# A fill tile per token block between late levels of the triangular solver, instead of behind the right-hand sides

## The reference

```python
def step(state, inp):                       # rwkv7_scan
    r_t, w_t, k_t, v_t, a_t, b_t = inp
    sa = jnp.einsum('bhij,bhj->bhi', state, a_t)
    state = (state * w_t[:, :, None, :] + sa[..., None] * b_t[:, :, None, :]
             + v_t[..., None] * k_t[:, :, None, :])
    return state, jnp.einsum('bhij,bhj->bhi', state, r_t)

m = jnp.where(strict, jnp.einsum('bnhid,bnhjd->bnhij', k_beta, k) * decay_mat, 0.0)
t_inv = lax.linalg.triangular_solve(eye + m, jnp.broadcast_to(eye, m.shape), left_side=True,
                                    lower=True, unit_diagonal=True)   # chunk_gated_delta_rule
```

## Time and profile before

| | us |
|---|---|
| median of three runs | 3095.12 (3090.31 to 3096.48) |
| the profiled execution, own time | 3103.75 |
| its span | 3100.7 |
| TensorE matmuls busy | 2743.8 (88% of the span) |
| VectorE busy | 1880.1 (61%) |
| ScalarE busy | 1342.8 (43%) |
| mean granted TensorE clock | 0.925 of full speed |

### The profile page before, as it was taken

One profiled execution on the slowest core, in us unless ns is written; L12 is line 12 of the kernel. 1 busy time (PEld: TensorE's weight loads), 2 busy tenths in 40 slices (PEclk: granted clock), 3 DMA queues, 4 the chain that ended last, 5 costly groups with the idle time before them and its releaser, 6 DMA issues. The chain is left out here.

```text
span 3100.7 us, 58400 instructions
## 1 busy us (share of the span) xinstructions
PE 2743.8 (88%) x25404; PEld 2336.9 (75%) x25404; DVE 1880.1 (61%) x2644; ACT 1342.8 (43%) x1882; POOL 87.9 (3%) x120
## 2 busy tenths in 40 slices
PE   7887778999887688999998888889999988978899
PEld 6776656888776657898887775678888877757788
DVE  5755766975765766956656444656565655446564
ACT  5413334655413244645453232544454532325453
POOL 0020000000110000000000200000000011000000
PEclk9897889999997889999998888989999988889999
DMA  5211114564211123554542121335655421113353
GB/s 222 96 43 55 69 56 149 192 214 174 83 59 52 69 96 136 203 196 165 203 152 103 42 71 40 112 138 201 221 179 203 151 77 56 69 41 130 143 199 128
DMA packets 54686, 386.48 MB, mean 125 GB/s; under 512 B 6688, under 2 KB 7328, under 8 KB 8352
## 3 DMA queue, kind: packets, MB, share of 16 engines
q1 hardware_dynamic: 54432, 382.76, 34.7%
HBM read 381.69 MB, written 1.05 MB: 123 GB/s over the span
## 5 line engine op out<-in xcount | busy, mean ns | idle before, releaser
L321 PE MATMUL banks<-normed_high,weights_high 128*128 128x256 f16 (+1 forms) x4096 | 1141.6, 279 | 42.7 <-DVE weights_low L307 20.1
L322 PE MATMUL banks<-normed_low,weights_high 128*128 128x256 f16 (+1 forms) x4096 | 1140.2, 278 | 0.0
L323 PE MATMUL banks<-normed_high,weights_low 128*128 128x256 f16 (+1 forms) x4096 | 1139.7, 278 | 0.0
L307 DVE SCALAR_TENSOR_TENSOR weights_low<-weight_ring,weights_high 128x2048 f16<-128x2048 f32 x334 | 761.2, 2279 | 406.3 <-ACT weights_high L301 391.9
L301 ACT ACTIVATE weights_high<-weight_ring 128x2048 f16<-128x2048 f32 x306 | 580.2, 1898 | 274.8 <-PE banks L323 262.6
L321 PE MATMUL banks<-projected,weights_high 128*128 128x256 f16 x1696 | 472.3, 278 | 72.4 <-DVE projected L332 72.4
L321 PEld LDWEIGHTS banks<-normed_high,weights_high 128*128 128x128 f16 (+1 forms) x4096 | 409.7, 100 | 121.7 <-issue 30.2
L322 PE MATMUL banks<-projected,weights_high 128*128 128x256 f16 x1696 | 472.7, 279 | 0.0
L323 PE MATMUL banks<-projected,weights_low 128*128 128x256 f16 x1696 | 472.2, 278 | 0.0
L323 PEld LDWEIGHTS banks<-normed_high,weights_low 128*128 128x128 f16 (+1 forms) x4096 | 408.5, 100 | 55.8
L322 PEld LDWEIGHTS banks<-normed_low,weights_high 128*128 128x128 f16 (+1 forms) x4096 | 408.6, 100 | 55.5 <-issue 1.3
(11 more groups left out here) (398 smaller groups left out, 3021.2 us busy)
## 6 DMA issues: line engine op xcount, KB each, us to landing
weight_ring<-w SPq DMA_DIRECT2D x356, 1024.0 KB, 4.8
small_weights<-small SPq DMA_DIRECT2D x2, 1280.0 KB, 7.3
constants<-const SPq DMA_DIRECT2D x1, 1601.0 KB, 10.1
weight_ring<-w SPq DMA_DIRECT2D x2, 640.0 KB, 3.8
residual<-xt SPq DMA_DIRECT2D x1, 1024.0 KB, 4.8
small_weights<-small SPq DMA_DIRECT2D x2, 512.0 KB, 10.4
out<-residual SPq DMA_DIRECT2D x4, 256.0 KB, 2.5
parameters<-par SPq DMA_DIRECT2D x2, 115.5 KB, 9.4
```

The lines of the kernel that those rows point to most:

```text
L307: nc.vector.scalar_tensor_tensor(out=self.part(self.mem.w_low, g), in0=self.part(self.mem.ring, g), scalar=W_SCALE, in1=self.part(self.mem ...
L321: pe.matmul(out, w_high, high, start=start, stop=False, skip_group_check=skip)
L322: pe.matmul(out, w_high, low, start=False, stop=False, skip_group_check=skip)
L323: return pe.matmul(out, w_low, high, start=False, stop=stop, skip_group_check=skip)
```

## The change

In all four stages, one fill tile per block leaves its place in the chain behind the solver and goes between two levels of the solver: tile 2 (n = 0) and tile 6 (n = 1), in rwkv behind level 4 in both blocks, in delta behind level 5 for n = 0 and behind level 4 for n = 1. These tiles now use PSUM bank 6 instead of 0. ScalarE copies them out from inside its part of the solver (behind level 5, in delta n = 0 behind level 6), and TensorE waits for these copies (`fill_out` 3 and 7) before the right-hand sides take bank 6. Behind `rhs` in rwkv, behind `new` in delta n = 0 and behind the seen part in delta n = 1 there is now no fill tile.

```diff
--- before.py
+++ after.py
@@ -1582,12 +1582,12 @@
                 say(A(bonus[:, i, :], bonus[:, i, :], ACT.Identity, bias=col("gn_b", i)),
                     "bonus_shifted")
             out(1)
-            solver.scalar(act, nc, sig, 0, {3: [high(3)]})
-            out(2, 3)
+            solver.scalar(act, nc, sig, 0, {3: [high(3)], 5: [lambda: out(2)]})
+            out(3)
             high(4)()
             out(4, 5)
-            solver.scalar(act, nc, sig, 1, {2: [lambda: norm.root(act, nc, say, 1)], 3: [high(5)]})
-            out(6)
+            solver.scalar(act, nc, sig, 1, {2: [lambda: norm.root(act, nc, say, 1)], 3: [high(5)],
+                                            5: [lambda: out(6)]})
             high(6)()
             out(7)
             norm.root(act, nc, say, 2)
@@ -1642,8 +1642,11 @@
                 solver.tensor(pe, sig, n, {0: [lambda pe: need("near_seen", 2),
                                                lambda pe: fill.tensor(pe, sig, 5)],
                                            "growth": [lambda pe: need("fill_out", 6)],
+                                           4: [lambda pe: fill.tensor(pe, sig, 6)],
                                            5: [lambda pe: norm.turn(pe, 1, TURN_BANK[0])]} if n
-                              else {"growth": [lambda pe: need("fill_out", 2)]})
+                              else {"growth": [lambda pe: need("fill_out", 2)],
+                                    4: [lambda pe: fill.tensor(pe, sig, 2)]})
+                need("fill_out", (3, 7)[n])
                 if n:
                     need("turned_read", 1)
 
@@ -1654,7 +1657,6 @@
                         mm = pe.matmul(o, p_k[hp(h), h % 4, b1], state[hp(h), h % 4, :],
                                        start=False, stop=True)
                 mm.then_inc(sig("rhs_summed"), 1)
-                fill.tensor(pe, sig, (2, 6)[n])
                 need("rhs", n + 1)
                 need("t_ready", 2 * len(LEVELS) * (n + 1))
                 for h in range(HEADS):
@@ -2765,14 +2767,15 @@
                     out(0, 1)
                     say(A(flat(y_out), flat(dz), ACT.Sigmoid), "z_sigmoid")
                     high(2)()
-                    solver.scalar(act, nc, sig, n, {2: [high(3)]})
-                    out(2, 3)
+                    solver.scalar(act, nc, sig, n, {2: [high(3)], 6: [lambda: out(2)]})
+                    out(3)
                     high(4)()
                 else:
                     out(4, 5)
                     solver.scalar(act, nc, sig, n, {2: [high(5)],
-                                                    3: [lambda: norm.root(act, nc, say, 1)]})
-            out(6, 7)
+                                                    3: [lambda: norm.root(act, nc, say, 1)],
+                                                    5: [lambda: out(6)]})
+            out(7)
             high(6)()
             norm.root(act, nc, say, 2)
             out(8, 9, 10, 11, 12, 13)
@@ -2790,6 +2793,7 @@
             for n in range(NBLK):
                 if n:
                     need("state", 1)
+                    need("fill_out", 3)
 
                 for s in range(HEADS):
                     o = ps[:, 2 + s // 4, (s % 4) * P:(s % 4 + 1) * P]
@@ -2809,23 +2813,25 @@
                 for i in ((0, 1), (4, 5))[n]:
                     fill.tensor(pe, sig, i)
                 need("fill_out", (2, 6)[n])
-                solver.tensor(pe, sig, n, {5: [lambda pe: norm.turn(pe, 1, TURN_BANK[0])]} if n
-                              else {})
+                solver.tensor(pe, sig, n, {4: [lambda pe: fill.tensor(pe, sig, 6)],
+                                           5: [lambda pe: norm.turn(pe, 1, TURN_BANK[0])]} if n
+                              else {5: [lambda pe: fill.tensor(pe, sig, 2)]})
                 if n:
                     need("turned_read", 1)
+                    need("fill_out", 7)
                     for s in range(HEADS):
                         mm = pe.matmul(ps[:, 6 + s // 4, (s % 4) * HD:(s % 4 + 1) * HD],
                                        kh[hp(s), s % 4, :], state[hp(s), s % 4, :],
                                        start=True, stop=True)
                     mm.then_inc(sig("seen_summed"), 1)
-                    fill.tensor(pe, sig, 6)
                 need("rhs", 2 * (n + 1))
                 need("t_ready", 2 * len(LEVELS) * (n + 1))
                 for s in range(HEADS):
                     mm = pe.matmul(ps[:, 4, s * HD:(s + 1) * HD], tt[:, s, :],
                                    rhs[:, s * HD:(s + 1) * HD], start=True, stop=True)
                 mm.then_inc(sig("new_summed"), 1)
-                fill.tensor(pe, sig, (2, 7)[n])
+                if n:
+                    fill.tensor(pe, sig, 7)
                 need("new", n + 1)
                 for s in range(HEADS):
                     o = ps[:, 4 + s // 4, (s % 4) * HD:(s % 4 + 1) * HD]
@@ -2859,8 +2865,8 @@
 
 
 AHEAD = 2
-RWKV_BANKS = (3, 2, 0, 2, 2, 3, 0, 2, 1, 3, 0, 2, 1)
-DELTA_BANKS = (0, 1, 0, 0, 0, 1, 0, 1, 2, 3, 0, 1, 2, 3)
+RWKV_BANKS = (3, 2, 6, 2, 2, 3, 6, 2, 1, 3, 0, 2, 1)
+DELTA_BANKS = (0, 1, 6, 0, 0, 1, 6, 1, 2, 3, 0, 1, 2, 3)
 HGRN_SLOTS = (2,) + (1, 1, 0) * 2 + (1, 0, 0, 2, 1)
 DSA_SLOTS = (4,) + (1, 0, 0) * 4
 FOX_SLOTS = (1, 1, 0) * 4
```

## The result

The changed kernel took 3113.1 us (median of seven runs, 3111.3 to 3118.1); seven runs of the kernel before took 3102.6 (3090.3 to 3104.0). The ratio is 1.0048 (95% interval 1.0035 to 1.0062), some 15 us slower; forecast were 13.6. The two medians stand only 10.5 us apart, for the seven runs of before fall into two groups, three at 3090.3 to 3096.5 and four at 3102.6 to 3104.0; the ratio lies between what either group alone would give (19 and 10 us). The two profiled executions stand 15.5 us apart: span 3116.2 us after and 3100.7 before, mean granted clock 0.922 and 0.925.

What follows compares the result with a forecast made beforehand. TensorE was taken as the bound, by its own rate or a TensorE-ScalarE-VectorE chain, its varying clock mattering most. Terms -8.0 + 25.4 - 1.8 - 2.0 = +13.6 us gave 3108.7 us; eight-in-ten range 3096 to 3119.

Steps and rivals of the forecast that it cites:

- Tiles out, tiles in: Eight fill tiles leave their places behind the right-hand sides, -32.6 us; put between solver levels they cost +14.5 us.
- Waits: Behind the right-hand sides TensorE now waits uncovered for VectorE's copy: 1.06 us in six blocks, 1.87 in two; +10.1 us.
- The half clock carried on: Clock lost around level 6 returns only in tile 3 or 7, slowing T·rhs, state and that tile; 29.2 us, weighed +25.4.
- The weight of 0.87: Factor on the 29.2 us of carried half clock, for blocks that do not fall or fall later; gives +25.4 us.
- L2825 at full clock in half of the cases: Delta n = 0: with the tile directly ahead of level 6, these 16 matmuls may run at full clock; -1.8 us.
- the pairs L2797/L2799: Delta: a later clock rise lets more of the 16 pairs run fast; 4.8 us per stage at most, -2.0 us taken.
- the clock falls where it fell: Rwkv and delta n = 1: a whole level separates new tile and level 6, so the fall does not move.
- Constant clock: Rival: the fall no longer reaches T·rhs or costs nothing new; +3.6 us, 3098.7 us; chance 0.13.
- The late fill holds the clock: Rival: a tile nearer level 6 keeps the clock up through the right-hand sides; -20 us in all eight blocks; chance 0.10.
- VectorE takes the bound: Rival: behind `rhs`, one more low half is uncovered in four n = 1 blocks; +9 us on top, 3118 us; chance 0.11.
- The rule of the Trainium skill: Long idle gaps between matmul bursts drop the clock, continuous busy time restores it; no gap here would be long enough.
- the second rival: "The late fill holds the clock"; argued against because level 6 read 1.0 in two rows, the clock falling only behind it.

Runs made afterwards that it cites:

- delta_only: The change made in the two delta stages alone, rwkv as in the kernel before; 3102.0 us, ratio 1.0015 to the kernel before.
- rwkv_only: The change made in the two rwkv stages alone, delta as in the kernel before; 3106.1 us, ratio 1.0028 to the kernel before.
- next_first: Changed kernel with tile 3 or 7 moved one step forward, into the place that tiles 2 and 6 had; 3115.3 us, ratio 1.0056 to the kernel before.
- dummy_tile: Changed kernel plus 24 unused matmuls of a fill tile's shape in each of the eight old tile places; 3116.6 us, ratio 1.0063 to the kernel before.
- three_tiles: Kernel before with a third tile inside each n = 1 block, ahead of level 5, and one tile less at the block's end; 3101.7 us, ratio 1.0011.
- after_hold: Changed kernel plus five unused matmuls in each of level 6's two holes and eight in the uncovered wait; 3109.2 us, ratio 1.0037 to the kernel before.

## Why the prediction was right

The mechanism was right: a half clock carried on from the right-hand sides to the next tile. Its sum goes through the trace of the kernel after as follows, each line over the eight blocks.

*Tiles out, tiles in.* -32.6 us holds for this pair of traces, being read from before. It is no typical value: the first block's 5.12 us was 2.62 in delta_only with the same program. The new tiles took 2.72 us from their start to that of the level (862.12 to 864.85), all eight at full clock and none late for its weights or bank; +14.5 as forecast.

*Waits.* 0.85 us of idle TensorE, and the tile used to begin 0.16 us ahead of the modelled end of the right-hand sides (875.12, and 873.28 + 2.00): 1.0 against 1.06. L1552 does the releasing in rwkv. In delta n = 1 VectorE's low half stands ahead of the adds, as foreseen. VectorE's timeline there, after:

```profile
1802.17 2.29 DVE L589 SCALAR_TENSOR_TENSOR weights_low<-weight_ring,weights_high 128x2048 f16<-128x2048 f32 x1
1804.38 0.87 DVE L2731 TENSOR_TENSOR scratch<-scratch,banks 128x256 f32<-128x256 f32 x2
```

TensorE waits for it for 2.16 us there and for 0.97 in the second layer, where the right-hand sides themselves were slow; forecast were 1.87 each. Together 9.2 us against 10.1.

*The half clock carried on.* The heart of the forecast, +25.4 us, was sized well: the T·rhs of rwkv and of delta n = 1 and the outputs of delta n = 0 all went from 1.90 or 2.00 to 3.67 (14.0 in all), the state of delta n = 0 from 0.97 to 1.60 (1.3 instead of 1.7), and the next tiles took 35.0 us from start to start instead of 21.4 (13.7 instead of 13.3): 29.0 us, all of what had been priced. The weight of 0.87 was too low by 3.6 us. It allowed for a block that would go on without a fall, and there was none: the second rwkv layer's n = 0 fell at 871.28.

*Given back.* Here two terms were off, in opposite directions. "L2825 at full clock in half of the cases", -1.8 us, failed: with both holes of level 6 filled by a dense tile the clock still fell at 1745.10 and 2588.19, in the microsecond ahead of T·rhs. The idea was that a dense tile right ahead protects what follows; it didn't over 2.3 us of level 6 and 1.2 us of idle time. The other, -2.0 us for the pairs L2797/L2799, was the right place and too small. Where the clock came back later here, the next fall mostly came later too. In all stretches behind the tile (the pairs, and the last outputs of n = 1) half clock shrank by 13.7 us net, in the first layer's pairs alone from 10.2 to 3.4, worth some 6.8 us.

*Not in the sum.* In two rwkv and two delta blocks the first fall moved too: the right-hand sides of the second rwkv layer took 3.67 instead of 2.00 and 9.95 instead of 8.75, those of delta n = 1 1.60 instead of 2.00 and 2.88 instead of 1.60. Net +3.8 us. For rwkv n = 0 this is more than the chance of one trace. With the tile between the levels and nothing in level 6 (after, rwkv_only, next_first, dummy_tile) the clock fell in the last matmuls of level 6 in all eight such blocks, and the right-hand sides took 3.67 us each time. With the tile at its old place (before, delta_only, three_tiles) it fell ahead of T·rhs in two of six, and the other four took 48.1 us. So the tile's new place itself brings the fall forward. The prediction had that at nothing ("the clock falls where it fell"); why it does so isn't shown.

Sum: -32.6 + 14.5 + 9.2 + 29.0 + 3.8 - 6.8 = +17.1 us, against 16.3 read from the blocks. Most of the 0.8 between them is level 6 of the second delta layer's n = 0: from its first matmul to T·rhs it took 5.09 us before, partly at half clock, and 3.50 after, 0.7 more off than in the first layer. Outside of the blocks another 0.8 came off. So the forecast of 13.6 was near for the right reason, but its nearness is in part luck: errors of 3.6 (weight), 1.8 (L2825) and 3.8 (earlier falls) one way and of 0.9 (waits), 4.8 (pairs) and 0.8 (level 6) the other cancel. And both traces stray. Against the rwkv blocks of delta_only the changed ones cost 16.6 us instead of the 9.6 against before, where the runs of rwkv_only say 0.28%, 8.7 us.

*Rivals.* "Constant clock" is refuted in size: no T·rhs kept its clock, and after_hold shows 0.4 us of 6.4 as that part in one block. By the mean clocks of the runs (0.9263 to 0.9227, at 2.1 us for each 0.001) the clock costs 7.6 us, which with +3.6 makes 11 of the 15; by the two traces it is 12.3 of 15.5, which leaves 3.2. What the other 4 us of the runs are isn't shown; after_hold leaves about as much open. "The late fill holds the clock" is refuted by delta n = 0 and by the eight T·rhs at 0.50. "VectorE takes the bound": in the uncovered waits TensorE stood idle for 0.85 to 2.16 us, and the one low half in the way was in the sum already, at 1.87 us. The rule of the Trainium skill that the prediction weighed (page "TensorE: Matmul & The Clock Gate", section "Why this matters for your kernels") would have given +3.6 us; the trace after disagrees with it once more, since the slow tile 3 at 880.08 follows a T·rhs without any idle time.

What the prediction missed altogether is the better change. The same reading of level 6 that foretold the loss also said where to mend it, and 80 unused matmuls there gave 0.4%. Its argument against the second rival read the earlier trace rows wrong in one place: of the two level-6 rows at 1.0 only the second has a fall behind it; in the block of the first (870.19) the clock didn't fall at all. And it blamed the thin stretch behind level 6 alone, while in the trace of before the clock fell inside level 6 in the first block (at 185.35), and filling level 6's holes put the fall off.

## What to carry to other kernels

Before a dense piece of filler is moved into a hole, look at what the clock does around its old place: if the granted clock rises in it, it pays for all that follows, and here the hole filled elsewhere didn't make up for that. Where a clock is lost in sub-microsecond holes of a thin stage, fill those holes with something dense, unused matmuls if need be, and keep the real tiles where they raise the clock. And settle such a change by the times of many runs, with their mean clock beside them, and by the same block in several traces, those of other variants too where its program is the same: one pair of traces moves by as much as the effect, and the mean clock alone would have called after_hold as fast as before.

## What the runs showed of the hardware

A stretch of small float32 matmuls can hold half clock without one idle nanosecond, and the same piece of the program can run at either clock. In the part behind the second delta layer, which no kernel here changed, the kernel before fell to half for 3.4 us and the changed one for 17.1. Windows of it after, with a row of its timeline (a head's pair of 64-row matmuls, L1968):

```profile
2735.00:2752.00 17.00, 17.00 (x51) 9.79 (x50) 5.59 (x19) 4.12 (x13) 0.00 (x0) 0.50 0.00 1
```

```profile
2736.81 1.22 PE L1968 MATMUL banks<-projected 64*128 64x256 f32 x2
```

and the same pair in the kernel before, where it is L1966:

```profile
2726.21 0.70 PE L1966 MATMUL banks<-projected 64*128 64x256 f32 x2
```

The fall came 8 us earlier in the program than before, and nothing in the stretch, 17.00 us busy of 17.00, brought the clock back until 2752.03. That alone is 7.6 us in this pair of traces; four of the ten traces have it (7.5 to 8.9 us), a fifth 5.7 us, and five none. It is one way in which a change of one stage shows up in another that it doesn't touch.

Time without idling did not bring the clock back by itself here. Of the 53 rises in the trace of the kernel before, 39 fall in matmuls of L321, L322 and L323, fill tiles and other projections of the same form. That form has 44% of TensorE's half-clock busy time in that trace and 74% of the rises, so this count alone is a weak sign. The experiments say more: all eight sets of 24 unused matmuls in dummy_tile have a rise in them, and in none of the ten traces does one fall in the right-hand sides, the seen part, T·rhs, outputs or state of rwkv or delta (up to 48 small float32 matmuls in a row without idle time). The other 14 rises of before do fall in float32 matmuls, in eleven other lines (two in the 64x64 ones of the solver's long levels, two each in L1987 and L2368). So the type isn't all of it either, and these runs don't say what is.
